# First attention of a two-block model: mask product in fp32r, and value products of two query head pairs in one visit

## The reference, cut to what matters

```python
# T = 1024 tokens, Lc = 256 context tokens, 8 query heads, 2 key/value heads of 64, BLOCK = WINDOW = 128
def window_ctx_attention(q, k, v, kc, vc, sink):
    ...
    s_win = jnp.einsum('bnqhgd,bnkhd->bhgnqk', qb, kw).astype(jnp.float32) * scale
    qpos = jnp.arange(NB)[:, None, None] * BLOCK + jnp.arange(BLOCK)[None, :, None]
    kpos = (jnp.arange(NB)[:, None, None] - 1) * BLOCK + jnp.arange(3 * BLOCK)[None, None, :]
    valid = (jnp.abs(qpos - kpos) <= WINDOW) & (kpos >= 0) & (kpos < T)
    s_win = jnp.where(valid, s_win, -jnp.inf)
    s_ctx = jnp.einsum('bnqhgd,bchd->bhgnqc', qb, kc).astype(jnp.float32) * scale
    ...
    p = jax.nn.softmax(jnp.concatenate([s_win, s_ctx, s_sink], axis=-1), axis=-1)
    ...
    out = (jnp.einsum('bhgnqk,bnkhd->bnqhgd', p_win, vw)
           + jnp.einsum('bhgnqc,bchd->bnqhgd', p_ctx, vc))
    return out.reshape(B, T, H * dh)
```

## Time and profile before

| | |
|---|---|
| time, median of 3 runs | 2757.99 us |
| the runs | 2753.02 to 2762.81 us |
| span of the profiled execution, first to last instruction | 2754.1 us |
| mean granted TensorE clock over the span | 0.979 |
| attention, layer 0, first scores to last values | about 482 to 639 us |
| attention, layer 1 | about 1274 to 1410 us |
| instructions | 37985 |

### The profile page before, as it was taken

One profiled execution on the slowest core, in us unless ns is written; L12 is line 12 of the kernel. 1 busy time (PEld: TensorE's weight loads), 2 busy tenths in 40 slices (PEclk: granted clock), 3 DMA queues, 4 the chain that ended last, 5 costly groups with the idle time before them and its releaser, 6 DMA issues. The chain is left out here.

```text
span 2754.1 us, 37985 instructions
## 1 busy us (share of the span) xinstructions
PE 2615.1 (95%) x14960; PEld 2162.6 (79%) x14960; DVE 1722.1 (63%) x2651; ACT 1055.9 (38%) x2001; POOL 826.5 (30%) x570
## 2 busy tenths in 40 slices
PE   6999999999999999999989989999999999989998
PEld 4789888788866799888878768866587888868886
DVE  4312475677544512775765554958847777699997
ACT  3201223665622401234656334268724222233331
POOL 0000100234631000101326410026312666576664
PEclk8999999999999999999999999999999999999999
DMA  7322322136655312321356431100300444544441
GB/s 285 97 89 80 80 80 70 41 94 200 203 218 181 141 60 83 92 87 59 70 161 196 153 137 47 42 16 1 129 29 27 154 157 151 181 168 135 147 154 68
DMA packets 183103, 314.10 MB, mean 114 GB/s; under 512 B 29346, under 2 KB 110932, under 8 KB 176912
## 3 DMA queue, kind: packets, MB, share of 16 engines
q1 hardware_dynamic: 161776, 296.93, 32.3%
q10 hardware_dynamic: 21152, 14.75, 1.7%
HBM read 235.47 MB, written 70.92 MB: 111 GB/s over the span
## 5 line engine op out<-in xcount | busy, mean ns | idle before, releaser
L1032 PE MATMUL ps<-xn_hi_sb,ft_hi_sb 128*128 128x512 f32 (+1 forms) x720 | 263.5, 366 | 1.0 <-DVE ft_lo_sb L1483 1.0
L1034 PE MATMUL ps<-xn_hi_sb,ft_lo_sb 128*128 128x512 f32 (+1 forms) x720 | 262.9, 365 | 0.0
L1033 PE MATMUL ps<-xn_lo_sb,ft_hi_sb 128*128 128x512 f32 (+1 forms) x720 | 262.9, 365 | 0.0
L984 PE MATMUL ps<-tm_hi_sb,xn_hi_sb 128*128 128x512 f32 (+2 forms) x608 | 216.7, 356 | 15.3 <-DVE xn_lo_sb L1397 7.3
L986 PE MATMUL ps<-tm_hi_sb,xn_lo_sb 128*128 128x512 f32 (+2 forms) x608 | 213.7, 352 | 0.0
L985 PE MATMUL ps<-tm_lo_sb,xn_hi_sb 128*128 128x512 f32 (+2 forms) x608 | 213.6, 351 | 0.0
L1032 PEld LDWEIGHTS ps<-xn_hi_sb,ft_hi_sb 128*128 128x128 f32 x720 | 136.8, 190 | 23.4 <-DVE ft_lo_sb L1483 1.4
L1033 PEld LDWEIGHTS ps<-xn_lo_sb,ft_hi_sb 128*128 128x128 f32 x720 | 136.7, 190 | 21.5
L1034 PEld LDWEIGHTS ps<-xn_hi_sb,ft_lo_sb 128*128 128x128 f32 x720 | 136.5, 190 | 21.6
L2291 POOL TENSOR_TENSOR arena_sb<-arena_sb 128x1024 f32<-128x1024 f32 x10 | 25.7, 2569 | 418.8 <-ACT arena_sb L2006 418.8
L2087 ACT ACTIVATE arena_sb<-ps,neg_max_sb 128x640 f32<-128x640 f32 (+1 forms) x144 | 109.2, 758 | 104.2 <-DVE neg_max_sb L1650 101.1
(11 more groups left out here) (517 smaller groups left out, 7437.3 us busy)
## 6 DMA issues: line engine op xcount, KB each, us to landing
arena_sb<-in_w_ft SPq DMA_DIRECT2D x44, 512.0 KB, 3.5
arena_sb<-mqk_dram SPq DMA_DIRECT2D x36, 512.0 KB, 3.6
hq_dram<-h_part_sb SPq DMA_DIRECT2D x14, 1280.0 KB, 4.8
arena_sb<-x_dram SPq DMA_DIRECT2D x33, 512.0 KB, 7.2
arena_sb<-in_w_ada SPq DMA_DIRECT2D x16, 1024.0 KB, 9.0
d_raw_sb<-in_w_down SPq DMA_DIRECT2D x16, 1024.0 KB, 5.8
xn_raw_sb<-hq_dram SPq DMA_DIRECT2D x30, 512.0 KB, 3.7
u_raw_sb<-in_w_up SPq DMA_DIRECT2D x16, 768.0 KB, 4.3
```

The lines of the kernel that those rows point to most:

```text
L984: pe.matmul(at, hi, tm_hi[b][:, k, :], start=k == 0, stop=False)
L1032: pe.matmul(to, hi, xn_hi_flat[:, k, at:at + size], start=k == 0, stop=False)
L1033: pe.matmul(to, hi, xn_lo_flat[:, k, at:at + size], start=False, stop=False)
L1034: mm = pe.matmul(to, lo, xn_hi_flat[:, k, at:at + size], start=False, stop=k == KT - 1)
```

## The change

The mask goes to the chip as fp32 (three variants of 256 columns, 393 KB in place of 197 KB), is converted in place to fp32r by POOL after its last rope piece, and the mask product takes an fp32r identity in place of the bf16 one. TensorE waits for that conversion (`a_mask_r`) ahead of attention. There are four pairs of turned buffers, one for each pair of heads, and the values of pairs 2 and 3 of the block before are taken together at h = 1, those of pairs 0 and 1 at h = 5. In the last block of a layer pair 2 is taken at h = 7 and pair 3 at the end, as before.

```diff
-    o["wmask"] = (o["wmask"].view(np.uint32) >> 16).astype(np.uint16)
...
-        ident_bf = sb("ident_bf", [P, P], BF16)
+        ident_r = sb("ident_r", [P, P], F32R)
...
-        prob_t = [[part(XL + 3776 + NKEY * (2 * u + g), NKEY // P, P) for g in range(KV)] for u in range(2)]
+        prob_t = [[part(XL + 3776 + NKEY * (2 * u + g), NKEY // P, P) for g in range(KV)] for u in range(4)]
...
-        wmask = part(ACC + 7576, 3 * P).bitcast(BF16).rearrange("p (b k) -> p b k", b=3)
+        wmask_raw, wmask = apart("wmask_raw", ACC + 7576, 3, 2 * P), rounded("wmask", ACC + 7576, 3, 2 * P)
...
-                    sp.dma_start(wmask, A["wmask"].bitcast(BF16).rearrange("p b e k -> p b (e k)")).then_inc(a_mask[l], 16)
+                    sp.dma_start(wmask_raw, A["wmask"].rearrange("p b e k -> p b (e k)")).then_inc(a_mask[l], 16)
...
                 def attention(l):
-                    pe.wait_ge(a_mask[l], 16)
+                    pe.wait_ge(a_mask_r, 1)
...
-                            pe.matmul(ends, ident_bf[:, :], wmask[:, edge, :].rearrange("p (t n) -> p t n", t=2), start=False, stop=False)
+                            pe.matmul(ends, ident_r[:, :], wmask[:, edge, :].rearrange("p (t n) -> p t n", t=2), start=False, stop=False)
...
-                                               prob_t[j % 2][g][:, n, :], start=n == 0, stop=n == n_all - 1)
+                                               prob_t[j][g][:, n, :], start=n == 0, stop=n == n_all - 1)
...
+                        before = WIN if b <= NX else 0
                         for h in range(HEADS):
                             turn(s0 + h, h, n_win)
...
                             if h == 1 and later:
-                                values(b - 1, 3, 0 if isinstance(b, int) and b > NX else WIN)
+                                values(b - 1, 2, before)
+                                values(b - 1, 3, before)
                             if h == 2 and b > by_dma:
                                 spread_inverse(b - 1, 1 - u)
-                            if h == 3 and later:
-                                pe.wait_ge(a_gated[l], b)
-                            if h >= 3 and h % 2:
-                                values(b, h // 2 - 1, n_win)
+                            if h == 5:
+                                if later:
+                                    pe.wait_ge(a_gated[l], b)
+                                values(b, 0, n_win)
+                                values(b, 1, n_win)
+                            if h == 7 and next_win is None:
+                                values(b, 2, n_win)
...
+                    pool.wait_ge(a_mask[l], 16)
+                    pool.tensor_copy(wmask, wmask_raw).then_inc(a_mask_r, 1)
```

More of the change, by code:

```diff
@@ L606, in first_block_layer @@
             g_act_chain = {l: Chain(sem("g_act_chain"))}
-            a_mask = sem_per_layer("a_mask")
+            a_mask, a_mask_r = sem_per_layer("a_mask"), sem("a_mask_r")
             a_az = sem_per_slot("a_az")
@@ L1333, in setup @@
                     dve.wait_ge(const_ld, CONST_ALL)
-                    dve.tensor_copy(ident_bf[:, :], ident[:, :]).then_inc(setup_dve, 1)
+                    dve.tensor_copy(ident_r[:, :], ident[:, :]).then_inc(setup_dve, 1)
                     dve.tensor_scalar(neg_sink[:, :, :], sink[:, :, :], -1.0, None, ALU.mult).then_inc(setup_dve, 1)
@@ L1682, in query_block @@
                             n = turned(n_win)[0]
-                            dve.tensor_copy(prob_t[h // 2 % 2][h % 2][:, 0:n, :], ps[:, 4, 0:n * P].rearrange("p (n q) -> p n q", n=n))\
+                            dve.tensor_copy(prob_t[h // 2][h % 2][:, 0:n, :], ps[:, 4, 0:n * P].rearrange("p (n q) -> p n q", n=n))\
                                 .then_inc(a_t_dve[l], 1)
@@ L2094, in query_block @@
                             m, n = turned(n_win)
-                            act.activation(prob_t[h // 2 % 2][h % 2][:, m:m + n, :], ps[:, 5, 0:n * P].rearrange("p (n q) -> p n q", n=n), ACT.Copy)\
+                            act.activation(prob_t[h // 2][h % 2][:, m:m + n, :], ps[:, 5, 0:n * P].rearrange("p (n q) -> p n q", n=n), ACT.Copy)\
                                 .then_inc(a_t_act[l], 1)
```

## The result

The changed kernel takes 2775.87 us (median of 4 runs, 2771.57 to 2778.19) against 2757.04 us of the kernel before in the same comparison: ratio 1.0071, 95% interval 1.0057 to 1.0084, 18.8 us slower. The forecast was 2776.1. The profiled execution of the changed kernel took 2771.57 us, its span is 2769.8 us.

What follows compares the result with a forecast made beforehand. TensorE was taken as the bound, with 0.34 us of latency to spare. Terms 21.8 + 1.8 - 3.0 - 3.5 + 1.0 = +18.1 us gave 2776.1 us, 0.7% slower; range 2752 to 2792.

Steps and rivals of the forecast that it cites:

- The mechanism: Window blocks: two heads of four have no values visit between scores and transposes; TensorE waits 1.07 us for the exponential.
- Part 1: Mask product in fp32r, 128 window heads: scores take 0.72 us instead of 0.80, 0.08 less each.
- the rival's loss: Mask product's fp32r weight load not hidden: scores 0.89 us, not 0.72, +9.5 us, 2786 us; chance 0.06.
- Part 2, the visits: Window blocks, two values visits joined: 2.31 us instead of 2.48, but exposed latency costs +21.8 us over 28 periods.
- The period: Four heads in the window blocks, one double visit to the next: 8.62 us against 7.84, +0.78.
- The +0.13 for the gating: VectorE's gating multiply after the double visit delays an uncovered reduction by 0.13 us in 14 blocks: +1.8 us.
- The stalls: Other stalls of the two window stretches, 7.8 us: a little under half falls into idle time, -3.5 us.
- Block 7's extra VectorE piece: A 1.48 us VectorE piece delays heads 6 and 7; the double visit covers it, -1.5 us per layer, -3.0.
- The first heads of block 0: These and the context blocks, where latency already rules: +1.0 us together, between -2 and +3.
- TensorE-bound: Rival: transposes after a double visit ready at 2.43, period 7.19 us, about 2734 us; chance 0.12.
- The clock: Rival: idling lowers the granted clock once per window block, 14 times: +24 us, 2800 us; chance 0.03.
- The weight load: Rival: the mask's fp32r weight load comes into the open, scores 0.89 us, 2786 us; chance 0.06.

Runs made afterwards that it cites:

- the two shorter chains: Row maximum over 256 context keys alone, or softmax scale in ScalarE's query copy: kernel before 2749.62 and 2755.72 us, changed kernel 2761.86 and 2765.36 us.
- the half visits: Kernel before with three of four values visits per block cut in two, each half behind its own head's scores: 2770.51 us, ratio 1.0048.

## Why the prediction was right, and where its parts were not

**The mechanism holds.** Two heads of four lost their cover, the first of them waits about 1 us (predicted 1.07, measured 1.0), the transposes then take 0.69 as foreseen, and the loss lies in the two window stretches. The run with the visits alone, the one with half the values left out and the two shorter chains, each worth more on the changed kernel than on the one before (14 against 7 us, 15 against 4), show it from different sides.

**Part 1 failed.** The prediction took scores from 0.80 to 0.72 because it laid the 0.26 us between the first product and the mask product to the bf16 weight load. With an fp32r mask the distance is still 0.26 (562.83 to 563.09 above). It belongs to the first product behind the transposes: where scores follow the projections' products it is shorter, in the changed kernel

```profile
482.21 0.34 PE L1073 MATMUL ps<-k_hi_sb,q_hl_sb 128*128 128x384 f32 x1
482.38 0.28 PE L1074 MATMUL ps<-wmask_sb,ident_r_sb 128*128 128x256 f32 x1
482.50 0.34 PE L1075 MATMUL ps<-k_lo_sb,q_hl_sb 128*128 128x384 f32 x1
```

(0.17), and in the kernel before it was 0.18 in the same place (482.41 to 482.59). From the first product's start to the fifth's it took 0.59 there in the changed kernel and 0.60 in the kernel before, against 0.68 behind transposes (562.83 to 563.51). The Trainium skill ("TensorE: Matmul & The Clock Gate", Weight-path perf modes) names the faster load of non-FP32 weights, and the trace agrees, 96 ns for the bf16 identity against 192 for the fp32r one. But in both kernels the loads run beside the products, so neither the forecast gain (28 x 4 x 0.08 = 9 us, partly inside waits) nor the rival's loss appeared. Why the first product behind transposes takes 0.09 more was not settled; the type of the transposes is not it (0.25 with fp32r transposes, 565.62 to 565.87).

**Part 2, the visits.** Double visit 2.31 predicted, 2.33 to 2.34 measured; transposes of the third head at 3.50 predicted, 3.57 measured. The Trainium skill ("TensorEngine Tiling (Array Packing)", Key Properties) says that a change of tiling mode drains the array. The 0.31 us per round trip of the half visits agrees with such a cost, though no run here shows that it is the drain. A gain of 0.3 could not pay for 1.0 of waiting.

**The period** was forecast at 8.62 and with the gating in every second one at 8.68; it is 8.86, 28 x 0.18 = 5 us more than forecast. Scores that take 0.79 in place of 0.72 lie three times on the path of a period, 0.21 us, the largest part of the miss. The +0.13 for the gating did not appear: since the scores took as long as before, the multiply was done when the reduction could start.

**The stalls.** The kernel before has 228.9 - 28 x 7.84 = 9.4 us of them in the stretches. The prediction let 5.0 vanish (3.5, and 0.73 ahead of head 6 in each layer); in the changed kernel every period of both layers lies between 8.75 and 8.95, so all 9.4 vanished. 4.4 us less than forecast. **The two misses cancel**: 28 x (8.86 - 7.84) - 9.4 = 19.1, where the prediction had 21.8 + 1.8 - 3.5 - 1.5 = 18.6 for the same stretches. The 2776.1 owes its closeness to that, which is luck.

**Block 7's extra VectorE piece.** Head 6 no longer waits behind the values, as forecast. Head 7 still comes late: its transposes start 1.47 us after head 6's, 1.80 before. The gain is 1.1 us per layer, not 1.5. The first heads of block 0, up to head 6, take 0.7 us more in layer 0 and 0.8 in layer 1, and the context blocks the same, where the forecast had +1.0 for all of them.

**The rivals.** TensorE-bound (2734) would have needed a latency of 1.9 us from scores to transposes; it is 3.05 (562.83 to 565.88). The clock stayed at 1.00 through the waits of the changed kernel's two stretches; a lower one shows in the run with half the values (0.97 in its stretch of layer 1). The weight load stayed hidden.

## What to carry to other kernels

Work of an engine that keeps it busy between an issue and its return is cover, and bundling it saves the switches and gives up the cover: count the latency from issue to use, and what stands in between for each item, before moving the filler. A busy share near 95% did not tell it; leaving out half of the filler did. And look at the clock when filler goes: the time that it frees can be taken back there. A gap beside an operation is only that operation's if it is missing where the operation stands behind something else.

## What was not expected of the hardware

- Leaving out 28 visits of about 1.5 us changed the time by a ratio of 0.9994, with a mean granted clock of 0.9755 instead of 0.9797.
- fp32r in place of bf16 for the identity doubles its weight load (96 to 192 ns) and changes the five products by 0.01 us (0.60 to 0.59).
- A round trip of TensorE from products with 128 columns of weights to ones with 64 and back costs 0.31 us.
- On POOL the multiplication of 64x512 fp32 by a constant, in place, takes 1.49 us, the cast of as much to fp32r 0.60.
- fp32r transposes of 128x128 take about 0.09 each instead of 0.105: five take 0.46 instead of 0.52 behind the values.
